# Embedding stages of a two-layer trunk: where VectorE adds the gate bias and converts three weight units

## The chip, the cores and the metric

The kernel runs on one core of a Trainium2 chip. The metric is the device time of the whole program in microseconds. TensorE is named PE in the rows, VectorE DVE, ScalarE ACT, GpSimd POOL and SyncE SP.

## What is computed

A trunk of two layers over 640 tokens (512 prompt frames and 8 x 16 frames of running streams), width 1024, in float32. Each layer is a half SwiGLU channel mixer, a mixer (pooling in layer 0, stick-breaking attention in layer 1), a second half SwiGLU, and an embedding of per-layer inputs, each with a layer norm behind it:

```python
def post_mixer(x, m, p_i, i):
    x = layer_norm(ALPHA * x + m, ln_g[i, 1], ln_b[i, 1])
    x = half_ffn(x, i, 1)
    gate = jax.nn.sigmoid(x @ ple_w_gate[i] + ple_b_gate[i])
    e = p_i @ ple_w_proj[i]
    return layer_norm(ALPHA * x + gate * e, ln_g[i, 3], ln_b[i, 3])
```

The change touches the last three lines of this, which the kernel calls the embedding stage. It is run once in each layer.

## The kernel before

**Precision.** Every matrix product is made of three float32r products: high part by high part, low part of x by high part of w, high part of x by low part of w. So each operand is split: the high part is a rounded copy, the low part is the rest.

**Weights.** They come in units of 128 x 1024 elements (512 KB), numbered in the order of use; a stage's first unit is `st.u0`. SyncE loads a unit into one of three raw buffers (`RAWS = 3`). ScalarE's `cvt_to(limit)` writes the high parts of all units below `limit` that are still to be done into a ring of seven slots (`RING = 7`, line 1018), VectorE's `cvt_to` the low parts (line 1351). ScalarE waits for the load and for the ring slot's former unit to be used up; VectorE waits for ScalarE's part of the same unit. SyncE issues the load of a unit only when VectorE has converted the unit three before it (semaphore `w_split`, line 752):

```python
r = raw_at[key]
if r >= RAWS:
    sp.wait_ge(w_split, raw_released(load_order[r - RAWS]))
```

**Embedding stage.** The tokens stand in five tiles of 128 (`TILES`), the width in two halves, so there are ten outputs: n = 0 to 4 for the first half, 5 to 9 for the second. A half has four units of gate weights and one of projection weights (`per_dh` = 5); u0 to u0+4 are the first half's, u0+5 to u0+9 the second's, and u0+9 is the second half's projection. For each output TensorE makes a gate (24 matmuls) and a projection (6 matmuls); the order is gates 0 to 3, projections 0 to 3, then gate n and projection n by turns. VectorE adds the bias to the gate in PSUM (`add_bias(n)`, line 1658, into `e_act`, which has two buffers), ScalarE takes the sigmoid (`sigmoid(n)`, line 1268), VectorE multiplies by the projection (line 1376), adds it to x (line 1378) and takes statistics (line 1361). These last three are `evacuate(st, n)`. Gate n on TensorE waits for bias n-2, since the PSUM bank is the same, and projection n waits for product n-2. From output 5 on, each tile's second half completes a row of x, and the norm follows: VectorE centres it (line 1395), ScalarE takes the standard deviation, VectorE rescales it (line 1403).

**After the stage in layer 0** comes the gate-and-up stage of layer 1, whose units begin at u0+10. TensorE transposes each normalised tile of x (line 1823), ScalarE takes the high part (line 1038, `hi`), VectorE the low part (line 1432, `low`). Its first pass (tokens 0 to 383) uses u0+10 and u0+11, and then u0+12 and u0+13; the transposes of the last two tiles stand between. The pass over tokens 384 to 639 waits for the low part of the last tile (`piece_lo`). ScalarE's order there is: the conversions left from the embedding stage, the table load for Silu, the first Silu, `hi` of tile 3, the high part of the first product, `hi` of tile 4. GpSimd loads the next gain and bias rows (line 843) when the stage's last norm is done. Layer 1's embedding stage is the end of the program: the output is stored and no unit is left behind u0+9.

All orders are written out by hand, one in-order stream for each engine.

Of the kernel before, what the change touches and what calls it, by code (L numbers as in the profile page):

```python
# [24 lines left out]
TILES = TOKENS // P  # L25
# [17 lines left out]
RING = 7  # L43
# [147 lines left out]
def streaming_trunk(nc, x_prompt, x_sample, cache_k, cache_v, state_pool, p_prompt, p_sample, ln_g, ln_b, ffn_w1,  # L191
# [12 lines left out]
    with ExitStack() as ctx:  # L204
# [170 lines left out]
        for st in stages:  # L375
# [6 lines left out]
            if st.kind == "down":  # L382
                w = ffn_w2[st.layer, st.n].rearrange("(c p) f -> p c f", p=P)
                for dh in range(2):
                    for k in range(0, FH, 2):
                        n = min(2, FH - k)
# [29 lines left out]
        def slot_of(u):  # L416

            if first_qk <= u < first_out:
                return (u - first_qk) % QK_SLOTS
            return u % RING if u < first_qk else (u - first_out) % RING  # L420

        def cols_in(u):
            return unit_source[u][1] * unit_source[u][2]
# [11 lines left out]
        def raw_slot(u):  # L435
            return raw_at[u] % RAWS
# [14 lines left out]
        for st in stages:  # L451
# [11 lines left out]
            if st.kind in ("down", "out", "embed", "v"):  # L463
                n = {"down": 5, "out": 3, "embed": 3, "v": 3}[st.kind]
# [533 lines left out]
        def _(se):  # L998
            done = [0]

            def cvt_to(limit):

                while done[0] < min(limit, n_units):
                    u = done[0]
                    if u in pool_units:
                        se.wait_ge(w_scaled, pool_units.index(u) + 1)
                    else:
                        se.wait_ge(w_loaded[raw_slot(u)], load_count[u])
                    if slot_before[u] is not None:
                        se.wait_ge(*freed[slot_before[u]])  # L1010
                    elif u == first_out + QK_SLOTS:
                        se.wait_ge(z_full, NU * PAIRS)
                    elif u == first_out + QK_SLOTS + 1:
                        se.wait_ge(s_full, NU * PAIRS - 2)
                    elif u >= first_out:
                        se.wait_ge(pv_done, NU * PAIRS)
                        se.wait_ge(k_stored, 32 * PAIRS)
                    se.activation(ring[:, slot_of(u), 0, 0:cols_in(u)], raw[:, raw_slot(u), 0:cols_in(u)],  # L1018
                                  ACT.Copy).then_inc(w_hi_done, 1)
                    done[0] += 1  # L1020
# [197 lines left out]
            for st in stages:  # L1218
# [46 lines left out]
                if st.kind == "embed":  # L1265
                    def sigmoid(n):
                        se.wait_ge(e_bias, st.gate0 + n + 1)
                        se.activation(e_act[:, n % 2, :], e_act[:, n % 2, :], ACT.Sigmoid).then_inc(e_sig, 1)

                    se.preload_act_table(ACT.Sigmoid)  # L1270
                    sigmoid(0)
                    hi(prev, 3)
                    sigmoid(1)
                    hi(prev, 4)
                    cvt_to(st.u0 + st.per_dh)
                    for c in range(PLE // P):
                        p_hi_of(st, c)
                    cvt_to(st.u0 + RING)
                    for n in range(2, TILES):
                        if n == 4:  # L1280
                            cvt_to(st.u0 + RING + 2)
                        sigmoid(n)
                    cvt_to(st.u0 + st.per_dh + RING)
                    sigmoid(TILES)
                    for t in range(TILES):
                        if t == 3:
                            hi(st, t - 1)
                        deviation(st, t)
                        if t in (1, 2):
                            hi(st, t - 1)  # L1290
                        if t < TILES - 1:
                            sigmoid(TILES + t + 1)
                        if t == 3:
                            cvt_to(st.u0 + st.per_dh + RING + 1)
                    cvt_to(st.u0 + st.per_dh + RING + 4)
# [33 lines left out]
        def _(ve):  # L1329
# [10 lines left out]
            def cvt_to(limit):  # L1340

                while done[0] < min(limit, n_units):
                    u = done[0]
                    n = cols_in(u)
                    if u in pool_units:
                        ve.wait_ge(scale_loaded, 16)
                        ve.wait_ge(w_loaded[raw_slot(u)], load_count[u])
                        ve.tensor_tensor(raw[:, raw_slot(u), :], raw[:, raw_slot(u), :], scale_row,
                                         ALU.mult).then_inc(w_scaled, 1)
                    ve.wait_ge(w_hi_done, u + 1)  # L1350
                    ve.tensor_tensor(ring[:, slot_of(u), 1, 0:n], raw[:, raw_slot(u), 0:n],  # L1351
                                     ring[:, slot_of(u), 0, 0:n].bitcast(F32), ALU.subtract).then_inc(w_split, 1)
                    done[0] += 1
# [5 lines left out]
            def statistics(t, dh):  # L1359

                return ve.bn_stats(stats[:, t, 6 * dh:6 * dh + 6], x[:, t, dh * DH:(dh + 1) * DH])  # L1361
# [6 lines left out]
            def evacuate(st, n):  # L1368

                dh, t = divmod(n, TILES)  # L1370
                dst = x[:, t, dh * DH:(dh + 1) * DH]
                ve.wait_ge(acc_full, st.y0 + n + 1)
                if st.kind == "embed":
                    ve.wait_ge(e_sig, st.gate0 + n + 1)
                    e = e_act[:, n % 2, :]
                    ve.tensor_tensor(e, e, ps[:, 2 * (n % 2) + 1, :], ALU.mult).then_inc(e_prod, 1)  # L1376
                    ve.wait_ge(e_prod, st.gate0 + n + 1)
                    ve.scalar_tensor_tensor(dst, dst, ALPHA, e, ALU.mult, ALU.add).then_inc(x_upd, 1)  # L1378
                elif st.kind == "down" and st.half == 1:
                    ve.tensor_tensor(dst, dst, ps[:, n % 4, :], ALU.add).then_inc(x_upd, 1)  # L1380
                else:
                    ve.scalar_tensor_tensor(dst, dst, ALPHA, ps[:, n % 4, :], ALU.mult, ALU.add).then_inc(x_upd, 1)  # L1382
                if st.ln is not None:
                    ve.wait_ge(x_upd, st.y0 + n + 1)
                    if dh == 0:
                        statistics(t, 0)
                    else:
                        moments(t, statistics(t, 1))
# [212 lines left out]
            for st in stages:  # L1601
# [50 lines left out]
                if st.kind == "embed":  # L1652
                    def add_bias(n):
                        dh = n // TILES
                        if n == 0:
                            ve.wait_ge(bias_loaded, 16 * (st.layer + 1))
                        ve.wait_ge(eg_full, st.gate0 + n + 1)
                        ve.tensor_tensor(e_act[:, n % 2, :], ps[:, 2 * (n % 2), :], gate_bias[:, dh * DH:(dh + 1) * DH],  # L1658
                                         ALU.add).then_inc(e_bias, 1)

                    add_bias(0)
                    low(prev, 3)
                    add_bias(1)
                    low(prev, 4)
                    cvt_to(st.u0 + st.per_dh)
                    for c in range(PLE // P):
                        k = st.pt0 + c + 1
                        bank = piece_bank(k)
                        ve.wait_ge(piece_hi, k)
                        ve.tensor_tensor(p_lo[:, c, :], ps[:, bank:bank + 2, :].rearrange("p b n -> p (b n)")[:, 0:TOKENS],  # L1670
                                         p_hi[:, c, :].bitcast(F32), ALU.subtract).then_inc(piece_lo, 1)
                    cvt_to(st.u0 + RING)
                    for n in range(TILES):
                        if n == 4:
                            cvt_to(st.u0 + RING + 2)
                        if n >= 2:
                            add_bias(n)
                        evacuate(st, n)
                    cvt_to(st.u0 + st.per_dh + RING)
                    add_bias(TILES)  # L1680
                    for t in range(TILES):
                        evacuate(st, TILES + t)
                        if t < 3:
                            centre(st, t)
                            add_bias(TILES + t + 1)
                            rescale(st, t)
                            if t:
                                low(st, t - 1)
                        if t == 3:
                            low(st, t - 1)  # L1690
                            normalise(st, t)
                            add_bias(TILES + t + 1)
                            cvt_to(st.u0 + st.per_dh + RING + 1)
                    normalise(st, TILES - 1)
                    cvt_to(st.u0 + st.per_dh + RING + 4)
                if st.kind == "pool":
# [340 lines left out]
```

## Time and profile before

| | us |
|---|---|
| median of 3 runs | 2577.8 |
| lowest, highest | 2576.84, 2579.41 |
| profiled execution, its own time | 2579.34 |
| its span | 2577.6 |
| TensorE busy | 2544.2 (99%) |
| VectorE busy | 1107.8 (43%) |
| ScalarE busy | 816.1 (32%) |
| GpSimd busy | 142.4 (6%) |

The mean granted clock of TensorE is 0.994. A busy TensorE is one whose matmuls overlap in the records, not one at its peak. Times within the span are counted from its start. The first embedding stage runs from about 994 to 1069 us on TensorE, the second from 2496 us to the end of its matmuls near 2569.5.

### The profile page before, as it was taken

The numbers are of one execution on the slowest core, as the hardware profiler recorded it, in microseconds if no ns is written. First come the engines' busy times: TensorE is split into PE (matmuls) and PEld (weight loads), VectorE is DVE, ScalarE is ACT, GpSimd is POOL, SyncE is SP. The second block draws the span as 40 slices with busy tenths as digits, with TensorE's granted clock in tenths as the row PEclk, the third lists the DMA queues.
The fourth block names the chain that finished last, engine by engine and source line by source line (L and its number), as shares of the span: only waits on it lengthen the run. The fifth ranks groups of instructions, "written<-read, shape, count | busy, mean of one in ns | idle before, by whom it ended". The sixth has DMA issues, their size and how long they took to land.

```text
span 2577.6 us, 37679 instructions
## 1 busy us (share of the span) xinstructions
PE 2544.2 (99%) x16260; PEld 2302.7 (89%) x16260; DVE 1107.8 (43%) x1477; ACT 816.1 (32%) x1272; POOL 142.4 (6%) x199
## 2 busy tenths in 40 slices
PE   8999999999999999999999999999999999999998
PEld 8998998899989988899899988777776999899986
DVE  4223323662233236733233251666666733233267
ACT  4212221132222222532122122666665322122133
POOL 3000000100000000000000001222123000000000
PEclk9999999899999999999999999999999999999999
DMA  6213222322132222322232124687776331232121
GB/s 181 73 62 94 75 69 70 112 71 75 62 94 73 71 78 74 98 83 78 62 98 66 62 74 139 185 220 199 221 207 191 98 93 65 62 99 81 47 94 66
DMA packets 376757, 259.09 MB, mean 101 GB/s; under 512 B 10449, under 2 KB 339153, under 8 KB 376592
## 3 DMA queue, kind: packets, MB, share of 16 engines
q1 hardware_dynamic: 371488, 239.64, 31.9%
q0 software_dynamic: 5104, 17.04, 2.0%
q8 instruction: 129, 2.11, 0.3%
q14 instruction: 36, 0.29, 0.0%
HBM read 248.22 MB, written 8.42 MB: 100 GB/s over the span
## 4 chain that ended last, share of the span: by engine, by line
PE 94%; DVE 3%; ACT 2%; issue 1%; POOL 0%; DVEq 0%; POOLq 0%; ACTq 0%
PE ps L1749 85%; PE ps L516 5%; PE ps L548 2%; PE ps L1823 1%; PE ps L624 0%; ACT e_buf L1077 0%; DVE x L1378 0%; DVE e_act L1376 0%; DVE stats L1361 0%; DVE ring L1351 0%; DVE e_buf L1479 0%; ACT kc_t L1061 0%; ACT wt L1102 0%; DVE s_sum L1514 0%; DVE x L1395 0%
## 5 line engine op out<-in xcount | busy, mean ns | idle before, releaser
L1749 PE MATMUL ps<-xt_hi,ring 128*128 128x384 f32 (+1 forms) x6144 | 1340.3, 309 | 5.1 <-ACT ring L1018 2.1
L1749 PEld LDWEIGHTS ps<-xt_hi,ring 128*128 128x128 f32 x6144 | 1036.0, 190 | 14.2 <-issue 10.4
L1749 PE MATMUL ps<-xt_lo,ring 128*128 128x256 f32 (+1 forms) x3072 | 944.1, 309 | 0.0
L1749 PEld LDWEIGHTS ps<-xt_lo,ring 128*128 128x128 f32 x3072 | 583.5, 190 | 0.2
L1749 PE MATMUL ps<-ring,h_hi 128*128 128x512 f32 x1760 | 549.9, 392 | 0.0
L1018 ACT ACTIVATE ring<-raw 128x1024 fp32r<-128x1024 f32 x326 | 324.9, 1028 | 427.1 <-PE ps L1749 353.5
L1351 DVE TENSOR_TENSOR ring<-raw,ring 128x1024 fp32r<-128x1024 f32 x326 | 383.1, 1203 | 134.7 <-ACT ring L1018 130.2
L1749 PEld LDWEIGHTS ps<-ring,h_hi 128*128 128x128 f32 x1760 | 332.6, 189 | 68.9
L1613 DVE SCALAR_TENSOR_TENSOR act<-act,ps 128x384 f32<-128x384 f32 (+1 forms) x176 | 85.8, 488 | 670.8 <-PE ps L1749 670.8
L1749 PE MATMUL ps<-ring,h_lo 128*128 128x512 f32 x880 | 344.2, 391 | 0.0
L1239 ACT ACTIVATE h_hi<-act 128x384 fp32r<-128x384 f32 (+1 forms) x176 | 83.0, 471 | 629.6 <-DVE act L1613 629.6
L1749 PE MATMUL ps<-ring,xt_hi 128*128 128x512 f32 (+1 forms) x720 | 221.2, 382 | 1.1 <-DVE e_act L1658 0.8
L1749 PEld LDWEIGHTS ps<-ring,h_lo 128*128 128x128 f32 x880 | 166.4, 189 | 34.1
L1749 PEld LDWEIGHTS ps<-ring,xt_hi 128*128 128x128 f32 x720 | 133.8, 190 | 28.2 <-issue 1.9
L1233 ACT ACTIVATE act<-ps 128x384 f32<-128x384 f32 (+1 forms) x176 | 77.1, 438 | 243.7 <-PE ps L1749 241.8
L1749 PE MATMUL ps<-ring,xt_lo 128*128 128x512 f32 (+1 forms) x360 | 136.5, 379 | 0.0
L1619 DVE TENSOR_TENSOR h_lo<-act,h_hi 128x384 fp32r<-128x384 f32 (+1 forms) x176 | 86.5, 491 | 92.3 <-ACT h_hi L1239 92.3
L1382 DVE SCALAR_TENSOR_TENSOR x<-x,ps 128x512 f32<-128x512 f32 x50 | 34.2, 685 | 191.8 <-PE ps L1749 191.8
L1749 PEld LDWEIGHTS ps<-ring,xt_lo 128*128 128x128 f32 x360 | 68.3, 190 | 11.9
L1380 DVE TENSOR_TENSOR x<-x,ps 128x512 f32<-128x512 f32 x40 | 27.4, 685 | 114.5 <-PE ps L1749 114.5
L977 POOL TENSOR_TENSOR sp_lo<-e_buf,sp_hi 128x512 fp32r<-128x512 f32 (+1 forms) x48 | 66.4, 1387 | 174.0 <-ACT sp_hi L1087 174.0
L548 PE MATMUL ps<-ident,k_raw 128*128 128x128 f32 x512 | 70.8, 276 | 2.6 <-DVE k_tok L1449 0.9
(137 smaller groups left out, 1591.2 us busy)
## 6 DMA issues: line engine op xcount, KB each, us to landing
raw<-in_ffn_w_dram SPq DMA_DIRECT2D x256, 512.0 KB, 4.4
k_raw<-in_cache_k_dram SPq DMA_DIRECT2D x128, 256.0 KB, 4.9
v_raw<-in_cache_v_dram SPq DMA_DIRECT2D x128, 256.0 KB, 4.2
raw<-in_sb_w_in_dram SPq DMA_DIRECT2D x24, 512.0 KB, 5.8
raw<-in_ple_w_gate_dram SPq DMA_DIRECT2D x16, 512.0 KB, 4.4
g_b<-in_ln_g_dram POOLq DMA_DIRECT2D x8, 512.0 KB, 4.2
b_b<-in_ln_b_dram POOLq DMA_DIRECT2D x8, 512.0 KB, 5.6
raw<-in_ffn_w_dram SPq DMA_DIRECT2D x16, 256.0 KB, 3.4
```

Source lines behind the costliest of these rows:

```text
L516: return pe.matmul(out, w, xx, start=start, stop=True, skip_group_check=True)
L548: ins = pe.transpose(ps[:, bank, kb * P:(kb + 1) * P], k_raw[:, sample % 2, j, kb, :], ident[:])
L977: pool.tensor_tensor(sp_lo[:, h, at:at + n], e_buf[:, g % 2, 0:n], sp_hi[:, h, at:at + n].bitcast(F32), ALU.subtract).then_inc(sp_lo_done, 1)
L1018: se.activation(ring[:, slot_of(u), 0, 0:cols_in(u)], raw[:, raw_slot(u), 0:cols_in(u)], ACT.Copy).then_inc(w_hi_done, 1)
L1233: se.activation(act[:, PART[p]], ps[:, 2 * ((n - 1) % 2), 0:PART[p].stop - PART[p].start], ACT.Silu).then_inc(act_done, 1)
L1239: se.activation(h_hi[:, i, PART[p]], act[:, PART[p]], ACT.Copy).then_inc(h_hi_done, 1)
L1351: ve.tensor_tensor(ring[:, slot_of(u), 1, 0:n], raw[:, raw_slot(u), 0:n], ring[:, slot_of(u), 0, 0:n].bitcast(F32), ALU.subtract).then_inc ...
L1380: ve.tensor_tensor(dst, dst, ps[:, n % 4, :], ALU.add).then_inc(x_upd, 1)
L1382: ve.scalar_tensor_tensor(dst, dst, ALPHA, ps[:, n % 4, :], ALU.mult, ALU.add).then_inc(x_upd, 1)
L1613: ve.scalar_tensor_tensor(act[:, PART[p]], act[:, PART[p]], 0.5, ps[:, 2 * ((n - 1) % 2) + 1, 0:PART[p].stop - PART[p].start], ALU.mult, A ...
L1619: ve.tensor_tensor(h_lo[:, i, PART[p]], act[:, PART[p]], h_hi[:, i, PART[p]].bitcast(F32), ALU.subtract).then_inc(h_lo_done, 1)
L1749: return pe.matmul(out, w, xx, start=first, stop=last, skip_group_check=True)
```

## The change

VectorE's code of the embedding stage is written in another order: the bias of tile n+2 is added after output n for n = 0 and 1, where the bias of tile n was added just before output n for n = 2 and 3. At the fourth tile both engines' `cvt_to` goes one unit further, so that three units (u0+7 to u0+9) are converted there and two (u0+10, u0+11) behind tile 4. On VectorE alone, the `cvt_to` for unit u0+12 between the bias of tile 9 and its product is taken out, and the one behind the last norm then does four units, u0+12 to u0+15. ScalarE converts u0+12 where it did.

```diff
@@ ScalarE, embedding stage
                     for n in range(2, TILES):
                         if n == 4:
-                            cvt_to(st.u0 + RING + 2)
+                            cvt_to(st.u0 + RING + 3)
                         sigmoid(n)
@@ VectorE, embedding stage
-                    for n in range(TILES):
-                        if n == 4:
-                            cvt_to(st.u0 + RING + 2)
-                        if n >= 2:
-                            add_bias(n)
+                    for n in range(4):
                         evacuate(st, n)
+                        if n < 2:
+                            add_bias(n + 2)
+                    cvt_to(st.u0 + RING + 3)
+                    add_bias(4)
+                    evacuate(st, 4)
                     cvt_to(st.u0 + st.per_dh + RING)
@@
                             normalise(st, t)
                             add_bias(TILES + t + 1)
-                            cvt_to(st.u0 + st.per_dh + RING + 1)
                     normalise(st, TILES - 1)
```

VectorE, first half of the stage in layer 0, outputs 1 to 4 and the conversions around tile 4. Before:

```order
L1376 TENSOR_TENSOR e_act<-e_act,ps 128x512
L1378 SCALAR_TENSOR_TENSOR x<-x,e_act 128x512
L1361 BN_STATS stats<-x 128x6
L1658 TENSOR_TENSOR e_act<-ps,gate_bias 128x512
L1376 TENSOR_TENSOR e_act<-e_act,ps 128x512
```

The same place, from output 0's statistics on, in the changed kernel:

```order
L1361 BN_STATS stats<-x 128x6
L1658 TENSOR_TENSOR e_act<-ps,gate_bias 128x512
L1376 TENSOR_TENSOR e_act<-e_act,ps 128x512
L1378 SCALAR_TENSOR_TENSOR x<-x,e_act 128x512
L1361 BN_STATS stats<-x 128x6
```

The first product in the upper piece is output 1's, with the bias of tile 2 behind its statistics; in the lower one this bias stands ahead of output 1's product.

ScalarE, both embedding stages, the conversions (line 1018) and sigmoids (line 1268) around tile 4; the first piece is layer 0's:

```order
 L1268 ACTIVATE e_act<-e_act 128x512 x2
-L1018 ACTIVATE ring<-raw 128x1024 x2
-L1268 ACTIVATE e_act<-e_act 128x512
 L1018 ACTIVATE ring<-raw 128x1024 x3
+L1268 ACTIVATE e_act<-e_act 128x512
+L1018 ACTIVATE ring<-raw 128x1024 x2
 L1268 ACTIVATE e_act<-e_act 128x512
```

Two conversions, tile 4's sigmoid and three more have become three, the sigmoid and two. VectorE's conversions of the same units move in the same way.

VectorE, end of the stage in layer 0, from the bias of tile 9 to the low part of tile 3 for the next stage. Before:

```order
L1658 TENSOR_TENSOR e_act<-ps,gate_bias 128x512
L1351 TENSOR_TENSOR ring<-raw,ring 128x1024
L1376 TENSOR_TENSOR e_act<-e_act,ps 128x512
L1378 SCALAR_TENSOR_TENSOR x<-x,e_act 128x512
L1361 BN_STATS stats<-x 128x6
L1366 BN_AGGR mv<-stats 128x2
L1395 SCALAR_TENSOR_TENSOR x<-x,mv,g_b 128x1024
L1401 RECIPROCAL rstd<-std 128x1
L1403 SCALAR_TENSOR_TENSOR x<-x,rstd,b_b 128x1024
L1351 TENSOR_TENSOR ring<-raw,ring 128x1024 x3
L1432 TENSOR_TENSOR xt_lo<-ps,xt_hi 128x8x128
```

In the changed kernel:

```order
L1658 TENSOR_TENSOR e_act<-ps,gate_bias 128x512
L1376 TENSOR_TENSOR e_act<-e_act,ps 128x512
L1378 SCALAR_TENSOR_TENSOR x<-x,e_act 128x512
L1361 BN_STATS stats<-x 128x6
L1366 BN_AGGR mv<-stats 128x2
L1395 SCALAR_TENSOR_TENSOR x<-x,mv,g_b 128x1024
L1401 RECIPROCAL rstd<-std 128x1
L1403 SCALAR_TENSOR_TENSOR x<-x,rstd,b_b 128x1024
L1351 TENSOR_TENSOR ring<-raw,ring 128x1024 x4
L1432 TENSOR_TENSOR xt_lo<-ps,xt_hi 128x8x128
```

The single conversion behind the bias (unit u0+12) has joined the three behind the last norm.

## Rows read from the trace of the kernel before

**Rows 1.** Page, part 4: shares of the chain that ended last, by engine.

```profile
PE 94%; DVE 3%; ACT 2%; issue 1%; POOL 0%; DVEq 0%; POOLq 0%; ACTq 0%
```

**Rows 2.** Timeline, TensorE, layer 0's stage: start, us, what, count [idle before <-releaser].

```profile
1021.97 0.99 PE L1749 MATMUL ps<-ring,p_hi 128*128 128x512 f32 x2
...
1024.51 0.50 PE L1749 MATMUL ps<-ring,xt_hi 128*128 128x512 f32 x1 [0.38 <-DVE e_act L1658]
...
1037.91 0.47 PE L1749 MATMUL ps<-ring,p_hi 128*128 128x512 f32 x1 [0.86 <-DVE ring L1351]
...
1079.49 1.09 PE L1823 MATMUL ps<-ident,x 128*128 128x128 f32 x8 [0.78 <-DVE x L1403]
...
1088.59 0.45 PE L1749 MATMUL ps<-xt_hi,ring 128*128 128x384 f32 x2
```

**Rows 3.** Timeline, VectorE, first half of layer 0's embedding stage.

```profile
1021.74 0.67 DVE L1376 TENSOR_TENSOR e_act<-e_act,ps 128x512 f32<-128x512 f32 x1
...
1023.78 0.67 DVE L1658 TENSOR_TENSOR e_act<-ps,gate_bias 128x512 f32<-128x512 f32 x1
...
1030.78 2.34 DVE L1351 TENSOR_TENSOR ring<-raw,ring 128x1024 fp32r<-128x1024 f32 x2
...
1036.55 2.35 DVE L1351 TENSOR_TENSOR ring<-raw,ring 128x1024 fp32r<-128x1024 f32 x2
```

**Rows 4.** Timeline, layer 1's embedding stage: one row of TensorE, one of VectorE.

```profile
2540.71 0.47 PE L1749 MATMUL ps<-ring,p_hi 128*128 128x512 f32 x1 [0.86 <-DVE ring L1351]
...
2561.43 0.69 DVE L1658 TENSOR_TENSOR e_act<-ps,gate_bias 128x512 f32<-128x512 f32 x1 [1.11 <-PE ps L1749]
```

**Rows 5.** Timeline, VectorE, end of layer 0's stage and start of the next.

```profile
1070.86 0.68 DVE L1658 TENSOR_TENSOR e_act<-ps,gate_bias 128x512 f32<-128x512 f32 x1
1073.19 1.23 DVE L1351 TENSOR_TENSOR ring<-raw,ring 128x1024 fp32r<-128x1024 f32 x1 [1.65 <-ACT ring L1018]
1074.33 0.68 DVE L1376 TENSOR_TENSOR e_act<-e_act,ps 128x512 f32<-128x512 f32 x1
...
1078.14 1.29 DVE L1403 SCALAR_TENSOR_TENSOR x<-x,rstd,b_b 128x1024 f32<-128x1024 f32 x1
...
1085.94 1.23 DVE L1432 TENSOR_TENSOR xt_lo<-ps,xt_hi 128x1024 fp32r<-128x1024 f32 x1 [1.51 <-ACT xt_hi L1038]
```

**Rows 6.** Timeline, ScalarE, the same place.

```profile
1076.95 2.94 ACT L1018 ACTIVATE ring<-raw 128x1024 fp32r<-128x1024 f32 x3
1079.90 1.28 ACT L1226 ACT_TABLE_LOAD   x1
```

**Rows 7.** Timeline, GpSimd, the same place: its two loads.

```profile
1079.72 0.53 POOL L843 DMA_DIRECT2D g_b<-in_ln_g_dram  x1 [79.95 <-DVE x L1403]
1080.24 0.53 POOL L843 DMA_DIRECT2D b_b<-in_ln_b_dram  x1
```

**Rows 8.** Line 758, SyncE's loads, in 1074:1075, then 1080:1082.3; time to landing.

```profile
L758 SPq DMA_DIRECT2D raw<-in_ffn_w_dram x1: 368/368/368, 1074.4 to 1074.4; - x1
DMA to landing us min/median/max: 3.9/3.9/3.9
...
L758 SPq DMA_DIRECT2D raw<-in_ffn_w_dram x2: 367/368/368, 1080.6 to 1081.7; - x2
DMA to landing us min/median/max: 7.2/7.5/7.9
```

**Rows 9.** Timeline, TensorE, end of the pool stage of layer 0.

```profile
525.79 1.09 PE L1823 MATMUL ps<-ident,x 128*128 128x128 f32 x8 [2.79 <-DVE x L1403]
528.05 2.93 PE L1749 MATMUL ps<-xt_hi,ring 128*128 128x384 f32 x8 [1.17 <-DVE x L1706]
530.78 1.77 PE L1749 MATMUL ps<-xt_lo,ring 128*128 128x384 f32 x8
532.38 1.55 PE L1749 MATMUL ps<-xt_hi,ring 128*128 128x384 f32 x8
```

**Rows 10.** Windows view of that stretch: busy us (x instructions) by engine, PEclk, DMA, GB/s.

```profile
528.00:532.00 4.00, 3.95 (x14) 3.95 (x15) 3.93 (x6) 0.29 (x1) 0.00 (x0) 0.60 0.00 0
```

## The prediction

> **What bounds the kernel now.** Read first the shares of the chain that ended last: TensorE holds 94% of the span [rows 1]. An edit on VectorE and ScalarE can pay only where TensorE stands still, so the view that matters is TensorE's timeline around the two embedding stages. In layer 0's stage it waits three times in plain sight [rows 2]: 0.38 us before tile 4's gate, for the gate bias of tile 2; 0.86 us before tile 5's projection, for a converted weight unit; 0.78 us before the last transposes of x, for the last norm. A fourth wait is hidden in the merged row at 1021.97: two matmuls take 0.99 us where such a pair takes 0.62, 0.37 us for VectorE's product of tile 1. Layer 1's stage repeats the 0.86 us wait [rows 4] and the first two; nothing follows its last norm. All this is about 3 us of 2578. A measurement of this kernel can tell about 0.2% (5.2 us) from no change, so the whole prize is smaller than that. What is left to ask is what the moves put at risk.
>
> **Bias two tiles ahead: nothing.** VectorE now adds tile 2's bias between tiles 0 and 1. TensorE's gate of tile 4 needs that bias, but the projection of tile 3, which stands ahead of it, needs the product of tile 1, and this starts one bias add later. VectorE's next start after a bias add comes 0.60 us later (its row lasts 0.67 us). Product of tile 1 before: 1021.74 + 0.67 = 1022.41 [rows 3]. Now: 1021.74 + 0.60 + 0.67 = 1023.01. The six matmuls of the projection take 1.5 us after a wait, so tile 4's gate could start at about 1024.56; before it started at 1024.51 [rows 2]. The 0.38 us wait has only moved ahead of the projection. I take +0.05 us; the bounds are -0.9 (both waits gone) and +0.6 (both stay).
>
> **Three conversions at the fourth tile: -1.1 us in each stage.** Before, the projection's unit u0+9 was the first conversion of the group at 1036.55, and TensorE waited for it [rows 2, 3]. Now it is the third of a group that starts near 1029.1, because the biases of tiles 2 and 3 are already done: 3 x 1.15 us end at 1032.5. TensorE comes to this projection at 1036.9, and to the gate that needs tile 4's bias (1033.1) at 1038.2. Both are ready. The saving is the 0.86 us idle and some 0.2 us to get going again, together 1.12; less the 0.05 above 1.07 us. Raw buffers are freed earlier too, so the next loads start 1 to 2 us sooner, into an idle stretch. In layer 1 VectorE waits 1.11 us for TensorE's gate of tile 8 [rows 4], so its tail after the last matmul follows: 1.07 us there too.
>
> **One conversion behind the last norm: a gain, then a larger loss.** Before, VectorE waited 1.65 us for ScalarE to convert unit u0+12, and then took 1.2 us for its own part, between the bias of tile 9 and its product [rows 5]. With that gone the product starts 1.46 us after the bias add (bias 0.6, sigmoid 0.63 and hand-overs), not 3.47 us. The last norm ended at 1078.14 + 1.29 = 1079.43. It now ends 2.01 us sooner by this and 1.07 by the step above, at 1076.35. TensorE comes to the transposes at about 1077.5: the 0.78 us wait is gone, 0.9 with the start-up. So TensorE runs ahead by 1.07 + 0.9 = 1.97 us. Unit u0+12 itself is in time: its conversion ends at 1077.5, and TensorE wants it at 1078.4.
>
> But a raw buffer is released by VectorE's part of the conversion. There are three, so the load of u0+15 is queued on SyncE behind the split of u0+12. Before, it was issued at 1074.4 and landed 3.9 us later [rows 8], and ScalarE's third conversion at the stage's end found it there: three in 2.94 us without a pause [rows 6]. Now it is issued at 1077.5. ScalarE's queue is strict: behind this conversion stand the table load for Silu, the first Silu, and the high parts of tiles 3 and 4 of x; VectorE's low parts wait for these; and TensorE's first pass over tiles 3 and 4, which began at about 1088.7 [rows 2], waits for the last low part.
>
> When does the load land? At the last norm's end GpSimd issues two 512 KB loads of gains and biases, 0.3 and 0.8 us after it [rows 7]. The trace has the very case: u0+16 was issued at 1080.6, 1.2 us after the last norm, behind those two loads, and took 7.2 us, the shorter of the two in its row [rows 8]. In the changed order u0+15 stands at exactly that place: 1.2 us after the norm, behind the same two loads, with the next ones as far behind it. So it lands at 1076.35 + 1.2 + 7.2 = 1084.75. The bounds are 3.9 (alone, as the load at 1074.4) and 7.9 (the load behind it, the longer of the two in that row); I take 7.2, since it has the same neighbours.
>
> The chain from there: ScalarE converts, 1.05 us, to 1085.8. Before, the table load began at 1079.90, as the third conversion ended [rows 6], and the last low part was done at 1085.94 + 1.23 = 1087.17 [rows 5], 7.27 us later. The same chain now ends at 1093.1. TensorE would be there at 1088.7 - 1.97 = 1086.7. It stands still for 6.4 us, and starts 4.4 us later than before.
>
> A pause of that size also costs clock. In the pool stage TensorE idled 2.79 us, ran eight transposes, and idled 1.17 us more; then the granted clock stood at 0.60 in the mean of the next 4 us, the lower level (1.2 GHz) for some 3.2 us of them, and the first two groups of eight matmuls took 2.93 and 1.77 us, where the third took 1.55 [rows 9, 10]. That is 2.93 + 1.77 - 2 x 1.55 = 1.6 us. The new pause is longer and unbroken, so I add 1.6, with bounds 0 (no fall) and 3.3 (the lower level lasts twice as long).
>
> A rule stands against the 7.2. The Trainium skill (Trainium Kernel Development and Optimization, Key Constraints) says that DMAs from SyncE's, ScalarE's and GpSimd's queues run on the same 16 engines and interleave. By that rule one load against two of its size would get half the engines and land no later than the second of them, which landed 5.8 us after 1080.24; the sum would be about 1.8 us smaller. The row agrees that they share the engines, but not that they share them evenly.
>
> **Sum.** Layer 0: +4.4 and +1.6; layer 1: -1.1. Together +4.9 us. The profiled execution took 2579.34 us (span 2577.6), 1.5 above the median of 2577.8. It would become 2584.2, and the median 2582.7, +0.19%.
>
> **Rivals.**
> *The clock stays low twice as long* after the pause, 3.3 us instead of 1.6. For it: the pause is 6.4 us where the pool stage's longest was 2.79. Against it: no row shows more than some 3.2 us at that level after a wait. It gives +6.6: 2584.4, slower by 0.26%. It decides from about 1.9 us of clock loss on.
> *The engines are shared evenly* and u0+15 lands after 5.4 us: +3.1, 2580.9. For it: both queues feed the same engines. Against: the 7.2.
> *The load is as fast as a lone one*, 3.9 us: pause 3.1 us, TensorE 1.1 us late, and 0 to 1.6 for the clock: 2577.8 to 2579.4. For it: the next loads behind it may be what slowed the row. Against: GpSimd's two come first.
> *No pause at all*, the gain that the order suggests: -1.97 and -1.07 give 2574.8, still within 0.2%. It would need the last low part before 1086.7, 6.4 us sooner than I find.
>
> **Chances.** Forecast 0.58, spread some 1 us about 2582.7 by the landing and the clock, so a part lies above 2583.0; clock twice as long 0.12; even sharing 0.12; lone speed 0.08; no pause 0.07; something unseen 0.03. Slower by over 0.2%: 0.40. Within: 0.57. Faster: 0.03. The range is 2578 to 2585: it leaves out the case without a pause, the far end of the clock, and the unseen.
>
> **What the profile of the changed kernel would show.** No wait for the projection's unit in either stage, and layer 1 about 1.1 us shorter from there on. A 0.6 us longer wait ahead of tile 3's projection in place of the one before tile 4's gate. The last norm's result ready before TensorE comes. Then ScalarE waiting about 7 us for a DMA into raw ahead of its last conversion of layer 0's stage, with a landing near 7 us, and TensorE idle some 6 us ahead of its first pass over tiles 3 and 4, followed by a stretch at the lower clock. I am wrong if ScalarE doesn't wait there, if the landing is near 4 us, or if TensorE has no pause over 3 us at layer 1's start.

## The result and the profile after

The changed kernel takes 2583.89 us in the median of 14 runs (2581.86 to 2585.10), the kernel before 2579.34 us (14 runs, 2576.84 to 2579.90). The ratio is 1.0021, with an interval of 1.0014 to 1.0028. The forecast was +4.9 us; +4.55 us between the medians and some 5.4 us by the ratio were measured.

Times within the two spans can't be compared as they stand: the profiled execution of the changed kernel comes to the first embedding stage 1.66 us earlier, in code that is the same in both. The start of the stage's first product on VectorE (line 1376) is the mark: 1019.68 in before, 1018.02 now. From this mark to the end of the span, before has 2577.6 - 1019.68 = 1557.9 us and the changed kernel 2581.2 - 1018.02 = 1563.2 us: +5.3. This "time from the mark" is used for every run below. It comes from one profiled execution of each kernel.

Who TensorE waited for, over the whole span of the changed kernel (us in total, times, longest):

```profile
PE ps L1749 <- DVE xt_lo L1432: 6.2, 1, 6.2
...
PE ps L1749 <- DVE e_act L1376: 1.4, 2, 0.7
```

The first row was not there before. The waits for the gate bias, for the second half's projection unit and for the last norm [rows 2, 4] are gone; two of 0.7 us for a product have come. The timeline of TensorE shows where (start, us, what, [idle before <-releaser]): the two waits for the product in layers 0 and 1, and the pause between them.

```profile
1021.40 0.50 PE L1749 MATMUL ps<-ring,p_hi 128*128 128x512 f32 x1 [0.70 <-DVE e_act L1376]
...
1091.25 0.58 PE L1749 MATMUL ps<-xt_hi,ring 128*128 128x256 f32 x1 [6.24 <-DVE xt_lo L1432]
...
2530.69 0.50 PE L1749 MATMUL ps<-ring,p_hi 128*128 128x512 f32 x1 [0.70 <-DVE e_act L1376]
```

The pass over tokens 384 to 639 starts at 1091.25, 73.23 us after the mark. Before, its first matmul was the second of the pair at 1088.59 [rows 2], near 1088.76 (0.12 us ahead of the next row, 1088.88), 69.1 us after the mark: it is now 4.1 us late. Why, is read on ScalarE's timeline at the same place:

```profile
1072.05 2.00 ACT L1018 ACTIVATE ring<-raw 128x1024 fp32r<-128x1024 f32 x2
1082.97 1.06 ACT L1018 ACTIVATE ring<-raw 128x1024 fp32r<-128x1024 f32 x1 [8.93 <-DMA raw<-in_ffn_w_dram]
1084.05 1.28 ACT L1226 ACT_TABLE_LOAD   x1
```

Three conversions in one go have become two, a wait of 8.93 us for the load of unit u0+15, and the third [rows 6]. The table load, and all that stands behind it, begins after that. VectorE's rows give the two ends of the chain:

```profile
1069.42 0.69 DVE L1376 TENSOR_TENSOR e_act<-e_act,ps 128x512 f32<-128x512 f32 x1 [0.77 <-ACT e_act L1268]
...
1073.24 1.28 DVE L1403 SCALAR_TENSOR_TENSOR x<-x,rstd,b_b 128x1024 f32<-128x1024 f32 x1
1074.44 3.49 DVE L1351 TENSOR_TENSOR ring<-raw,ring 128x1024 fp32r<-128x1024 f32 x3
1084.07 1.23 DVE L1351 TENSOR_TENSOR ring<-raw,ring 128x1024 fp32r<-128x1024 f32 x1 [6.13 <-ACT ring L1018]
...
1089.97 1.22 DVE L1432 TENSOR_TENSOR xt_lo<-ps,xt_hi 128x1024 fp32r<-128x1024 f32 x1 [1.50 <-ACT xt_hi L1038]
```

The last norm now ends at 1074.52, the load is issued after the first of the three conversions behind it, and the last low part is done at 1091.19. The load itself (line 758, the window 1074:1076), and GpSimd's two that were issued just before it:

```profile
L758 SPq DMA_DIRECT2D raw<-in_ffn_w_dram x1: 367/367/367, 1075.7 to 1075.7; - x1
DMA to landing us min/median/max: 7.3/7.3/7.3
...
1074.82 0.53 POOL L843 DMA_DIRECT2D g_b<-in_ln_g_dram  x1 [76.69 <-DVE x L1403]
1075.34 0.53 POOL L843 DMA_DIRECT2D b_b<-in_ln_b_dram  x1
```

And the granted clock (windows view: us, busy time of PE, PEld, DVE, ACT, POOL, then PEclk, DMA share, GB/s):

```profile
1088.00:1089.00 1.00, 0.00 (x0) 0.00 (x0) 0.47 (x2) 0.50 (x2) 0.00 (x0) 1.00 0.41 121
1089.00:1090.00 1.00, 0.00 (x0) 0.00 (x0) 0.03 (x1) 0.94 (x2) 0.00 (x0) 0.58 0.00 0
...
1095.00:1096.00 1.00, 1.00 (x7) 1.00 (x6) 0.59 (x1) 0.00 (x0) 0.00 (x0) 0.50 0.00 0
1096.00:1097.00 1.00, 1.00 (x10) 1.00 (x10) 0.00 (x0) 0.38 (x1) 0.00 (x0) 1.00 0.10 29
```

The clock fell near 1089.2, some 4 us into the pause, and was back at 1096.0. TensorE worked at the lower level from 1091.25 on, 4.75 us. Three matmuls of 256 columns lie from the start of one row below to the start of the next: 0.64 us for the first two rows, at the lower level, and 0.36 us for the last two, at full clock.

```profile
1091.62 0.41 PE L1749 MATMUL ps<-xt_lo,ring 128*128 128x256 f32 x1
...
1092.26 0.41 PE L1749 MATMUL ps<-xt_lo,ring 128*128 128x256 f32 x1
...
1096.06 0.28 PE L1749 MATMUL ps<-xt_lo,ring 128*128 128x256 f32 x1
...
1096.42 0.28 PE L1749 MATMUL ps<-xt_lo,ring 128*128 128x256 f32 x1
```

So 4.75 us of work would have taken 2.7: 2.1 us lost.

The first product of layer 1's embedding stage divides the rest, in the kernel before (first row) and the changed one (second row):

```profile
2522.48 0.69 DVE L1376 TENSOR_TENSOR e_act<-e_act,ps 128x512 f32<-128x512 f32 x1 [2.79 <-PE ps L1749]
...
2527.31 0.69 DVE L1376 TENSOR_TENSOR e_act<-e_act,ps 128x512 f32<-128x512 f32 x1 [2.80 <-PE ps L1749]
```

From the start of the pass over tokens 384 to 639 to this product, before took 1433.7 us and the changed kernel 1436.1: +2.3, of which the clock is 2.1. From this product to the end of the span it is 55.1 and 53.9: -1.2. So the +5.3 is made of +4.1, +2.3 and -1.2 (rounded).

### The profile page after: what moved, and what is told of

Read it like the earlier page. It is cut to its first block, busy times and chain, and to the rows that moved or that the text cites. A ratio compares the mean times of both kernels' runs of the same rounds, so it can differ in the third digit from the quotient of the medians.

```text
span 2581.2 us, 37679 instructions
## 1 busy us (share of the span) xinstructions
PE 2543.6 (99%) x16260; PEld 2303.5 (89%) x16260; DVE 1108.0 (43%) x1477; ACT 817.4 (32%) x1272; POOL 142.9 (6%) x199
## 4 chain that ended last, share of the span: by engine, by line
PE 95%; DVE 2%; ACT 2%; issue 1%; DMA 0%; POOL 0%; DVEq 0%; POOLq 0%; ACTq 0%
PE ps L1749 86%; PE ps L516 5%; PE ps L548 2%; PE ps L1823 1%; PE ps L624 0%; ACT e_buf L1077 0%; DVE e_buf L1479 0%; ACT kc_t L1061 0%; DMA raw<-in_ffn_w_dram 0%; ACT wt L1102 0%; DVE s_sum L1514 0%; DVE x L1395 0%; ACT xt_hi L1038 0%; DVE xt_lo L1432 0%; DVE e_act L1376 0%
```

## The experiments

The account under test: everything the change loses, it loses through one queued load. VectorE's conversion of u0+12 releases a raw buffer; behind the last norm it is done only 1.2 us after that norm; the load of u0+15 is issued then and takes 7.3 us to land; ScalarE's stream holds the next stage's first work behind this load. The rivals: VectorE's own queue (four conversions ahead of the low parts), or the first half's new order. Each run was timed in five rounds against the kernel before.

### The conversion put back

```diff
                             add_bias(TILES + t + 1)
+                            cvt_to(st.u0 + st.per_dh + RING + 1)
                     normalise(st, TILES - 1)
```

> The changed kernel with VectorE's conversion of unit u0+12 back ahead of output 9's product; the other two parts stay. My account (the loss comes from this part alone, through the load queued behind the split): the pause of 6.2 us at layer 1's start is gone, TensorE waits some 0.8 us for the last norm as before, and each stage keeps its 1.1 us: 2.1 us below before (0.9992). Rival (the first half's new order costs as well): at before's time or above, 1.0000 to 1.0010.

2575.55 us against 2578.38: ratio 0.9989 (0.9981 to 0.9998). From the mark 1555.6 us, 2.3 below before. The stage's one wait of TensorE behind the new 0.70 is the old one for the last norm, and ScalarE converts three units without a pause again:

```profile
1076.35 1.09 PE L1824 MATMUL ps<-ident,x 128*128 128x128 f32 x8 [0.78 <-DVE x L1403]
...
1073.81 2.94 ACT L1018 ACTIVATE ring<-raw 128x1024 fp32r<-128x1024 f32 x3
```

So the first half's new order is worth some 1.1 us in each stage, and the loss is all in the part that is undone here.

### The removal alone

```diff
                             add_bias(TILES + t + 1)
-                            cvt_to(st.u0 + st.per_dh + RING + 1)
                     normalise(st, TILES - 1)
```

This is the kernel before with nothing else changed.

> The kernel before with only the conversion of u0+12 moved behind the last norm. My account: the last norm ends 2.0 us earlier, the load of u0+15 is issued 1.2 us after it and lands 7 to 8 us later, TensorE's pause is about 6.3 us as in the changed kernel (both ends shift together) and 4.2 + 1.1 us of start plus 2.1 us of clock are lost: +7.4 us, 1.0029. Rival (the pause needs the first half's parts too): below +3 us, with a pause under 3 us.

2585.46 us against 2578.38: ratio 1.0026 (1.0016 to 1.0037). From the mark 2583.3 - 1018.07 = 1565.2 us: +7.3, where +7.4 was expected. TensorE and ScalarE:

```profile
1092.56 0.58 PE L1748 MATMUL ps<-xt_hi,ring 128*128 128x256 f32 x1 [6.27 <-DVE xt_lo L1432]
...
1084.29 1.06 ACT L1018 ACTIVATE ring<-raw 128x1024 fp32r<-128x1024 f32 x1 [8.97 <-DMA raw<-in_ffn_w_dram]
```

The same pause and the same wait as in the changed kernel. One line moved is the whole loss. The +7.4 of the expectation was met with one term too large: the pass starts 5.4 us late (1092.56 - 1018.07 = 74.5 us after the mark, before 69.1), and the stretch up to layer 1's first product is only 1.9 us longer, since the lower clock, which lasted from 1089.4 to 1096.2, reached 3.6 us into the work and not 4.75.

### The late unit left to the next stage

The changed kernel, with three conversions behind the last norm and not four, on both engines; u0+15 is then converted together with u0+16, behind the second product of the next stage.

```diff
-                    cvt_to(st.u0 + st.per_dh + RING + 4)
+                    cvt_to(st.u0 + st.per_dh + RING + 3)
```

The same line is changed on ScalarE and on VectorE.

> The changed kernel with unit u0+15 left to the next stage on both engines (three conversions behind the last norm, two behind the second product), so that nothing in front of the first Silu waits for its load. The load is issued at the same place. My account: no pause, no low clock there, TensorE keeps 1.97 us of layer 0 and 1.07 of layer 1: -3.0 us, 0.9988. Rival (VectorE's own queue of conversions ahead of the low parts makes the pause): one conversion less saves 1.1 us of it, so a pause of about 5 us stays, +4 us, 1.0016.

2574.32 us against 2578.38: ratio 0.9985 (0.9976 to 0.9994). From the mark 1554.7 us, 3.2 below before. The load is as slow as ever (7.3 us, issued at 1074.8), but nobody stands behind it. ScalarE:

```profile
1071.14 1.99 ACT L1018 ACTIVATE ring<-raw 128x1024 fp32r<-128x1024 f32 x2
1073.16 1.28 ACT L1226 ACT_TABLE_LOAD   x1
...
1085.24 2.00 ACT L1018 ACTIVATE ring<-raw 128x1024 fp32r<-128x1024 f32 x2
```

TensorE has no wait left at layer 1's start. The late conversion and the slow load are both still there, so neither makes the pause by itself: it takes the wait for this load ahead of the next stage's first work. The edit moves the unit on both engines, and so also takes one conversion out of VectorE's queue; the next run keeps all four there.

### GpSimd's loads held back

The changed kernel, with the two gain and bias loads issued after the last low part instead of after the last norm.

```diff
-                        pool.wait_ge(x_norm, st.norm0 + TILES)
+                        pool.wait_ge(piece_lo, st.piece_at(TILES - 1))
                         load_gb(norms[4])
```

> The changed kernel with GpSimd's two loads of gains and biases held until the last low part is done (some 13 us later), so that the load of u0+15 has the DMA engines to itself but for the units behind it. If the two loads are what makes it slow: it lands in about 4 us, the pause shrinks from 6.2 to about 3 us, TensorE starts its pass about 1 us later than in before, less or no low clock: 0 to +1.5 us, 1.0000 to 1.0006. Rival (the units behind it slow it, or VectorE's queue makes the pause): landing stays above 6.5 us or the pause above 5 us, +4 to +5 us, 1.0019.

2578.61 us against 2578.38: ratio 1.0002 (0.9993 to 1.0011). From the mark +1.5 us. TensorE, ScalarE, and the landing of u0+15 (line 758, the window 1074:1076):

```profile
1087.43 0.39 PE L1749 MATMUL ps<-xt_hi,ring 128*128 128x256 f32 x1 [3.05 <-DVE xt_lo L1432]
...
1079.15 1.06 ACT L1018 ACTIVATE ring<-raw 128x1024 fp32r<-128x1024 f32 x1 [5.73 <-DMA raw<-in_ffn_w_dram]
...
L758 SPq DMA_DIRECT2D raw<-in_ffn_w_dram x1: 367/367/367, 1075.1 to 1075.1; - x1
DMA to landing us min/median/max: 4.1/4.1/4.1
```

The landing falls from 7.3 to 4.1 us with the units behind it unchanged, and the pause from 6.24 to 3.05. VectorE has its four conversions here as in the changed kernel, and the pause became shorter by as much as the landing, so its queue is not the cause; the rival falls here, and with the run before. The units behind were still loaded behind it, so they are not what made it slow. The shorter pause still costs clock:

```profile
1087.00:1088.00 1.00, 0.57 (x5) 0.57 (x5) 0.84 (x2) 0.07 (x1) 0.33 (x1) 1.00 0.00 0
1088.00:1089.00 1.00, 1.00 (x10) 1.00 (x9) 0.55 (x1) 0.42 (x1) 0.72 (x2) 0.89 0.15 29
1089.00:1090.00 1.00, 1.00 (x7) 1.00 (x6) 0.41 (x2) 0.96 (x2) 0.00 (x0) 0.50 0.85 311
...
1092.00:1093.00 1.00, 1.00 (x10) 1.00 (x9) 0.00 (x0) 0.26 (x1) 0.00 (x0) 0.90 0.42 135
```

TensorE had been at work again for 1.35 us when the level fell, at 1088.8, and it stayed down for 3.4 us. The +1.5 us is made of 0.9 for the later start of the pass (70.0 us after the mark), 1.8 up to layer 1's first product (2522.92 in this run), and -1.2 from there on.

### The bias adds alone

The kernel before, with the biases of tiles 2 and 3 added two tiles ahead; all conversions in their old groups.

```diff
-                    for n in range(TILES):
-                        if n == 4:
-                            cvt_to(st.u0 + RING + 2)
-                        if n >= 2:
-                            add_bias(n)
+                    for n in range(4):
                         evacuate(st, n)
+                        if n < 2:
+                            add_bias(n + 2)
+                    cvt_to(st.u0 + RING + 2)
+                    add_bias(4)
+                    evacuate(st, 4)
```

> The kernel before with only the bias adds of tiles 2 and 3 moved two tiles ahead; the groups of conversions and the one before output 9's product as before. My account: TensorE's wait moves from tile 4's gate to tile 3's projection and the gate starts 0.05 us later; the conversion group at tile 4 starts 1.3 us earlier, but u0+9 still stands behind tile 4's bias and product. That part of it ends about 1.3 us earlier too, so of the 0.86 us wait before tile 5's projection most goes: -1 us in each stage, 0.9992. Rival (the bias move is worth nothing and the third conversion alone brings the gain): 1.0000, with the 0.86 us wait still there.

2576.22 us against 2578.49: ratio 0.9993 (0.9984 to 1.0002), an interval that includes no change; from the mark 1555.7 us, 2.2 below before. TensorE, then VectorE's second group with u0+9 at its head:

```profile
1022.04 0.50 PE L1750 MATMUL ps<-ring,p_hi 128*128 128x512 f32 x1 [0.70 <-DVE e_act L1376]
...
1033.80 2.34 DVE L1351 TENSOR_TENSOR ring<-raw,ring 128x1024 fp32r<-128x1024 f32 x2
```

The wait did move from the gate to the projection, as said. But the group with u0+9 starts 15.1 us after the mark (1018.66 in this run) where it stood 16.9 us after it in before [rows 3], and the 0.86 us wait is gone without any unit having changed its group.

### The third conversion alone

```diff
-                            cvt_to(st.u0 + RING + 2)
+                            cvt_to(st.u0 + RING + 3)
```

The same line is changed on ScalarE and on VectorE.

> The kernel before with only the third conversion taken to the fourth tile, on both engines. The group now ends near 1034.2, ahead of TensorE at 1036.9. My account: the 0.86 us wait is gone, the 0.38 us wait of tile 4's gate stays: -1.1 us in each stage, 0.9992. Rival (tile 4's bias is now late and makes a new wait before tile 6's gate at 1038.2; it would end at 1034.9): 1.0000.

2576.17 us against 2578.49: ratio 0.9990 (0.9982 to 0.9999). From the mark 1555.9 us, 2.1 below before. The bias wait is there, the unit's is not:

```profile
1024.08 0.50 PE L1749 MATMUL ps<-ring,xt_hi 128*128 128x512 f32 x1 [0.39 <-DVE e_act L1658]
...
1030.35 3.48 DVE L1351 TENSOR_TENSOR ring<-raw,ring 128x1024 fp32r<-128x1024 f32 x3
```

Each of the two parts saves about what both save together: 2.2, 2.1, and 2.3 us in the run with the conversion put back. The intervals of the ratios can't tell these from each other; the rows can, since the 0.86 us wait is gone in each. They are two cures for one wait.

### A version below both

The kernel that leaves u0+15 to the next stage, with the first two outputs in another order on VectorE.

```diff
-                    for n in range(4):
-                        evacuate(st, n)
-                        if n < 2:
-                            add_bias(n + 2)
+                    product(0)
+                    into_x(0)
+                    product(1)
+                    into_x(1)
+                    add_bias(2)
+                    first_stats(0)
+                    first_stats(1)
+                    add_bias(3)
+                    evacuate(st, 2)
+                    evacuate(st, 3)
```

`product`, `into_x` and `first_stats` are the three steps of `evacuate`.

> The kernel that leaves u0+15 to the next stage, with VectorE's first two outputs in another order: product 0, add 0, product 1, add 1, bias 2, statistics 0 and 1, bias 3. Product 1 is then ready at 2.1 us after product 0's start, before TensorE has done tile 2's projection, and tile 2's bias ends 0.3 us before its gate needs it. My account: the 0.70 us wait (0.97 with its start-up) goes in both stages: 1.9 us below the kernel that leaves u0+15 alone, 0.9978 of before. Rival (statistics moved back hold up the products of tiles 2 and 3, and the wait returns there): as the kernel without it, 0.9985.

2572.24 us against 2578.49: ratio 0.9977 (0.9968 to 0.9986). From the mark 2569.8 - 1017.18 = 1552.6 us, 5.3 below before. VectorE:

```profile
1017.18 0.69 DVE L1677 TENSOR_TENSOR e_act<-e_act,ps 128x512 f32<-128x512 f32 x1 [2.80 <-PE ps L1770]
1017.91 0.69 DVE L1682 SCALAR_TENSOR_TENSOR x<-x,e_act 128x512 f32<-128x512 f32 x1
1018.54 0.69 DVE L1677 TENSOR_TENSOR e_act<-e_act,ps 128x512 f32<-128x512 f32 x1
1019.26 0.69 DVE L1682 SCALAR_TENSOR_TENSOR x<-x,e_act 128x512 f32<-128x512 f32 x1
1019.87 0.68 DVE L1658 TENSOR_TENSOR e_act<-ps,gate_bias 128x512 f32<-128x512 f32 x1
```

Product 1 starts 1.36 us after product 0 (2.65 us in the changed kernel), and TensorE's list of waits has no row for the product, the bias or the last low part any more, and of the waits for a converted unit only one of 0.3 us is left, outside both embedding stages. That is 2.1 us below the kernel that leaves u0+15 alone, where 1.9 was expected.

## Why the prediction was right

The predicted 2582.7 us and +4.9 us stand against 2583.9 and +4.55 (+5.3 from the mark). The median of the kernel before rested on three runs; in fourteen it is 1.5 us higher, and this is why the forecast is low in absolute time and high in the difference of the medians. The path was right, and its terms were off by less than a microsecond each, with different signs. Step by step:

- **The load's place and its landing**, the term that turned a gain into a loss: 1.2 us after the last norm and 7.2 us by the row of u0+16 in before [rows 8]. Measured: 1075.7 - 1074.52 = 1.2 us, and 7.3 us. The row fitted because the same two loads of GpSimd stood in front; holding them back gave 4.1 us, near the lone load's price (3.9 in rows 8).
- **The chain behind it**: 7.27 us from the table load to the last low part; measured 1091.19 - 1084.05 = 7.14. TensorE's pause 6.4 us; measured 6.24. Start of the pass +4.4 us; measured +4.1.
- **The last norm 2.01 us earlier**: product of output 9 at 1.46 us after its bias add began; measured 1069.42 - 1067.97 = 1.45. Right, and worth nothing as long as the load queues behind it.
- **The clock**: 1.6 us by the pool stage, measured 2.1. The size was off, since the lower level lasted 4.75 us of TensorE's work and not 3.2; the row of the pool stage had been taken over without its being known at what point of the work the level comes back. The bounds (0 and 3.3) held it. In that stage the clock had in fact fallen before the window of rows 10 begins: 0.91 granted in 527 to 528, which puts the fall near 527.8 and makes the lower level 3.4 us long, 3.2 of them in TensorE's work. In the changed kernel it lasted 6.8 us, with 2.1 of them inside the pause. The matmuls after the pause lost another 0.2 us or so that the sum did not have.
- **Layer 1**: -1.1 us forecast; -1.2 measured from layer 1's first product to the end of the span.
- **Bias two ahead: nothing.** This step was right for its own wait and wrong as a price of the part. The 0.70 us wait came before tile 3's projection as worked out. But the prediction priced the part only by that, and gave the whole 1.1 us to the third conversion. The biases done early also take two 0.77 us waits for a sigmoid out of VectorE's stream, and so bring the next groups forward; alone they save 1.1 us in each stage, as the third conversion does alone. The sum did not suffer, since it counted the 1.1 us once.
- **The rule of even sharing**, weighed against the row, would have had u0+15 land after 5.4 us; it was 7.3. The row was right, and the even sharing did not show.
- **ScalarE's wait** was put at about 7 us and is 8.93: it had done its two conversions by 1074.05. The prediction gave no sum for that number. Its own times lead to 8.9: the two conversions, which in before begin at 1076.95, come 3.08 us earlier and end at 1075.8, and the load lands at 1084.75.
- **"About 3 us" for all waits, and a prize below 0.2%.** The four waits of layer 0 that the prediction lists are 2.4 us and the three of layer 1 are 1.6, together 4.0. The version without any of them is 5.3 us below before from the mark, ratio 0.9977 (0.9968 to 0.9986). So the prize was larger than said, about as large as the 5.2 us of the 0.2%. The forecast of this change did not use that number.

Of the rivals, the lone load's speed came true only when GpSimd's loads were out of its way, with a pause of 3.05 us for a forecast of 3.1. A case without a pause came true only by moving the wait for u0+15 into the next stage. In the rival of the clock the length was right, twice the pool stage's, and the price was not: the work lost 2.1 us and not 3.3, because part of the length fell in the pause.

Against the forecast of +0.19% and a chance of 0.40 for slower by over 0.2%, the ratio is 1.0021 with its interval on both sides of 1.002: the two cases were as close as the chances said.

## What to carry to other kernels

A step that converts or copies out of a ring of load buffers is also the release of a buffer. Before moving it, count the buffers, find the load that it lets go, and ask who will wait for that load and what stands behind the wait in that engine's stream. Here moving one conversion, whose unit TensorE had come to only 5.9 us after it was done, cost 7.3 us, because a load three units on was queued behind it and the next stage's first work behind that.

A price for such a load is best taken from a load of the same size with the same neighbours in front, not from the median: 3.9, 4.1, 7.2 and 7.3 us were all the price of 512 KB here. And when two edits both remove the same wait, each alone can show the full gain; run them one by one before adding them up.

## What the runs showed of the hardware that was not expected

The granted clock fell to its lower level (1.2 GHz) after a pause of 3.05 us, and only 1.35 us after TensorE had gone back to work; it came back 3.4 us later. After pauses of 6.24 and 6.27 us it fell 4.2 and 3.1 us into the pause, stayed low for 6.8 us in both, and so reached 4.75 and 3.6 us into the work. What a pause cost beyond the later start, up to layer 1's first product, was 2.3 us after 6.24 us, 1.9 after 6.27, and 1.8 after 3.05; the kernels without a pause differ by up to 0.2 us in this stretch. The price went with the work that fell into the lower level and not with the length of the pause.

Three loads of 512 KB issued within 1 us on two queues landed nearly in the order of issue and not together. In before these were 4.2 and 5.8 us for GpSimd's two and 7.2 us for SyncE's unit; the next unit took 7.9 us. Whether the engines took them in turn for a reason of the queues or of the addresses (GpSimd's loads repeat one row for all partitions) was not tried. A fourth raw buffer, which would let the load of u0+15 go without the conversion of u0+12, was not run either.
